# A row of indices placed in PSUM earlier, five banks for the gate's panels, and the level exponentials split over three iterations

## The reference, cut to what matters

```python
def peer_ffn(h, wq, keys, u, v):
    q = (xb @ wq).reshape(PEER_TOKEN_BLOCK, PEER_HEADS, 2, PEER_HALF_DIM)
    s = jnp.einsum('thpd,hpnd->thpn', q, keys)
    s1, i1 = lax.top_k(s[:, :, 0], PEER_TOPK)
    s2, i2 = lax.top_k(s[:, :, 1], PEER_TOPK)
    cand_s = s1[..., :, None] + s2[..., None, :]          # 16 x 16 candidates
    cand_i = i1[..., :, None] * PEER_N_KEYS + i2[..., None, :]
    top_s, pos = lax.top_k(cand_s, PEER_TOPK)
    idx = jnp.take_along_axis(cand_i, pos, axis=-1)
    gate = jax.nn.softmax(top_s, axis=-1)
    act = jax.nn.gelu(jnp.einsum('thkd,td->thk', u[idx], xb))
    return jnp.einsum('thk,thkd->td', gate * act, v[idx])
...
    ffn = peer_ffn(h, peer_wq[i], peer_keys[i], peer_u[i], peer_v[i])
    ple = jax.nn.sigmoid(h @ ple_gate_w[i]) * (p[i] @ ple_w[i])
    h = layer_norm(DEEPNORM_ALPHA * h + ffn + ple, ln2_g[i], ln2_b[i])
```

## Time and profile before

| | us |
|---|---|
| median of 3 runs | 3420.63 (3418.96 to 3421.29) |
| the profiled execution, its own time | 3419.54 |
| its span, first to last instruction | 3417.7 |
| PE busy | 3253.7 |
| DVE busy | 2574.4 |
| ACT busy | 1386.1 |
| POOL busy | 2071.9 |

### The profile page before, as it was taken

The page is one execution under the profiler, slowest core; times in us unless marked ns, Lnnn a source line. Parts: engine busy times, 40 slices in busy tenths (PEclk is TensorE's granted clock), DMA queues, the critical chain, the costliest instruction groups (busy, mean ns, idle before and its releaser), DMA issues. The chain is left out here.

```text
span 3417.7 us, 47046 instructions
## 1 busy us (share of the span) xinstructions
PE 3253.7 (95%) x17370; PEld 2905.1 (85%) x17370; DVE 2574.4 (75%) x4646; ACT 1386.1 (41%) x2698; POOL 2071.9 (61%) x1388
## 2 busy tenths in 40 slices
PE   5999899899999999999989998999999999999996
PEld 4777689899999988888777776899999999888885
DVE  5965359996875588888877733699869666988887
ACT  1235013366666433333212431144666664333332
POOL 5921677666677755555479035766666776555552
PEclk9999899999999999999989998999999999999998
DMA  3310224578899999999723012256888999999994
GB/s 121 94 61 15 95 77 151 195 293 300 296 332 347 350 388 368 363 360 359 254 75 98 32 50 86 75 180 208 295 304 299 344 355 357 384 365 361 361 361 156
DMA packets 312676, 817.12 MB, mean 239 GB/s; under 512 B 22272, under 2 KB 119552, under 8 KB 309120
## 3 DMA queue, kind: packets, MB, share of 16 engines
q1 hardware_dynamic: 112256, 349.02, 29.5%
q0 software_dynamic: 73728, 268.47, 20.2%
q10 hardware_dynamic: 126464, 196.63, 16.5%
HBM read 712.84 MB, written 101.19 MB: 238 GB/s over the span
## 5 line engine op out<-in xcount | busy, mean ns | idle before, releaser
L1239 POOL TENSOR_TENSOR u_lo<-panel,u_hi 128x1024 fp32r<-128x1024 f32 x256 | 629.2, 2459 | 339.8 <-ACT u_hi L1041 335.7
L588 PE MATMUL ps<-hT_hi,u_lo 128*128 128x384 f32 x2048 | 704.6, 344 | 9.1 <-POOL u_lo L1239 9.1
L588 PE MATMUL ps<-hT_lo,u_hi 128*128 128x384 f32 x2048 | 688.1, 336 | 0.0
L588 PE MATMUL ps<-hT_hi,u_hi 128*128 128x384 f32 x2048 | 688.0, 336 | 0.0
L588 PE MATMUL ps<-v_hi,w_lo 128*128 128x512 f32 x1536 | 597.7, 389 | 0.1
L588 PE MATMUL ps<-v_hi,w_hi 128*128 128x512 f32 x1536 | 597.5, 389 | 0.0
L588 PE MATMUL ps<-v_lo,w_hi 128*128 128x512 f32 x1536 | 597.5, 389 | 0.0
L1191 POOL TENSOR_TENSOR ring_hi<-panel,cst 128x512 fp32r<-128x512 f32 x244 | 276.3, 1132 | 441.5 <-PE ps L568 266.0
L1256 POOL TENSOR_TENSOR v_lo<-panel,v_hi 128x1024 fp32r<-128x1024 f32 x128 | 313.4, 2449 | 377.7 <-ACT v_hi L1103 377.6
L1103 ACT CAST v_hi<-panel 128x1024 fp32r<-128x1024 f32 x256 | 269.5, 1053 | 636.3 <-PE ps L588 624.8
L1041 ACT CAST u_hi<-panel 128x1024 fp32r<-128x1024 f32 x256 | 268.2, 1048 | 446.2 <-PE ps L588 441.0
(11 more groups left out here) (260 smaller groups left out, 5733.0 us busy)
## 6 DMA issues: line engine op xcount, KB each, us to landing
panel<-in_u SPq DMA_DIRECT2D x256, 512.0 KB
panel<-in_v SPq DMA_DIRECT2D x256, 512.0 KB
gate_scratch<-arena ACTq DMA_DIRECT2D x24, 2048.0 KB
act_scratch<-arena ACTq DMA_DIRECT2D x124, 384.0 KB
arena<-act_scratch ACTq DMA_DIRECT2D x62, 768.0 KB
arena<-gate_scratch ACTq DMA_DIRECT2D x62, 768.0 KB
panel<-in_w_in SPq DMA_DIRECT2D x28, 1024.0 KB, 5.2
panel<-in_wq SPq DMA_DIRECT2D x16, 1024.0 KB, 5.1
```

The costliest lines, as they stand in the source:

```text
L588: mm = nc.tensor.matmul(o, lhs[a], rhs[b_], start=(start and n == 0), stop=(stop and n == 2))
L1239: pr.mark(nc.gpsimd.tensor_tensor(u_lo[:, j % URING].rearrange("p c n -> p (c n)"), u_tile(j), u_hi[:, j % URING].rearrange("p c n -> p (c ...
```

## The change

Three edits, in both layers.

1. ACT copies `iota` into PSUM bank 3 right after the key scores, ahead of its copy of `x_rows`, and no longer at u tile 6. All four routings compare with `iota_ps`. DVE waits for the copy at the first comparison of each routing.
2. To leave bank 3 alone, the gate's eight outputs go through five banks: 0, 1, 2, 4, 5, 0, 1, 2. The sixth to eighth output wait for the sigmoids of the first to third. The first three u tiles wait for sigmoid 4, 5 and 6 in place of 5, 6 and 7.
3. The seven level exponentials of heads 1 to 3 are seven ACT instructions of 128x512. Levels 1 and 2 stand in the iteration with j % 4 = 1, levels 3, 4, 5 in the next, 6 and 7 in the one after, each right behind `fox_exps(2j)`. DVE signals levels 1 to 4 and 5 to 7 apart, and waits for them apart.

```diff
+SIGMOID_BANKS = (0, 1, 2, 4, 5)
...
+        LOW, HIGH = range(1, 5), range(5, LEVELS)
+        EXP_LEVELS = {1: (1, 2), 2: (3, 4, 5), 3: (6, 7)}
...
-        lev_ready = sig("lev_ready", HH)
-        lev_exp = sig("lev_exp", HH)
+        lev_ready = sig("lev_ready", 2 * HH)
+        lev_exp = sig("lev_exp", 2 * HH)
...
-                def take6(g, release):
+                def take5(g, release):
...
-                    if g >= 6:
-                        pr.need(*freed[g - 6])
+                    if g >= 5:
+                        pr.need(*freed[g - 5])
                     freed.append(release)
-                    return ps[:, g % 6, :]
+                    return ps[:, SIGMOID_BANKS[g % 5], :]
...
                     if j < 3:
-                        pe.wait_ge(gate_sig.sem, layer * gate_sig.per_layer + 5 + j)
+                        pe.wait_ge(gate_sig.sem, layer * gate_sig.per_layer + 4 + j)
...
-                def level_exps(hd):
-
-                    act.wait_ge(lev_ready.sem, layer * lev_ready.per_layer + hd + 1)
-                    for piece in zed_pieces(hd):
-                        last = nc.scalar.activation(piece, piece, ACT.Exp)
-                    pr.mark(last, lev_exp)
-
-                level_exps(0)
+                def level_exps(hd, levels):
+
+                    act.wait_ge(lev_ready.sem, layer * lev_ready.per_layer + 2 * hd + (1 if levels[-1] in LOW else 2))
+                    for lev in levels:
+                        last = nc.scalar.activation(zed(hd, lev), zed(hd, lev), ACT.Exp)
+                        if lev in (LOW[-1], HIGH[-1]):
+                            pr.mark(last, lev_exp)
+
+                act.wait_ge(lev_ready.sem, layer * lev_ready.per_layer + 2)
+                for piece in zed_pieces(0):
+                    last = nc.scalar.activation(piece, piece, ACT.Exp)
+                pr.mark(last, lev_exp, 2)
...
                     if j < NH:
                         fox_exps(2 * j)
+                        if j % NT in EXP_LEVELS and j // NT + 1 < HH:
+                            level_exps(j // NT + 1, EXP_LEVELS[j % NT])
...
-                    if j % NT == 1 and j // NT + 1 < HH:
-                        level_exps(j // NT + 1)
...
                 act.wait_ge(score_sb.sem, layer * score_sb.per_layer + 4 * NT)
+                pr.mark(nc.scalar.copy(iota_ps, iota), iota_ready)
                 pr.mark(nc.scalar.copy(x_rows, h[:, 0, :]), x_ready)
...
-                    pr.mark(nc.scalar.activation(ple_gate[:, i, :], ps[:, g % 6, :], ACT.Sigmoid), gate_sig)
+                    pr.mark(nc.scalar.activation(ple_gate[:, i, :], ps[:, SIGMOID_BANKS[g % 5], :], ACT.Sigmoid), gate_sig)
...
-                    if j == 6:
-                        act.wait_ge(gate_sig.sem, layer * gate_sig.per_layer + 8)
-                        pr.mark(nc.scalar.copy(iota_ps, iota), iota_ready)
...
-                    if levels[-1] == LEVELS - 1:
-                        pr.mark(last, lev_ready)
+                    pr.mark(last, lev_ready)
...
-                    dve.wait_ge(lev_exp.sem, layer * lev_exp.per_layer + hd + 1)
+                    dve.wait_ge(lev_exp.sem, layer * lev_exp.per_layer + 2 * hd + (1 if levels[-1] in LOW else 2))
...
-                        places = iota_ps if i > 1 else iota
+                        if a == 0:
+                            dve.wait_ge(iota_ready.sem, layer * iota_ready.per_layer + 1)
                         step(nc.vector.tensor_tensor(
-                            pick, places[:, 0:CAND].rearrange("p (o c) -> p o c", o=1).to_broadcast([P, TOPK, CAND]),
+                            pick, iota_ps[:, 0:CAND].rearrange("p (o c) -> p o c", o=1).to_broadcast([P, TOPK, CAND]),
...
-                dve.wait_ge(iota_ready.sem, layer * iota_ready.per_layer + 1)
```

More of the change, by code:

```diff
@@ L803, in _ @@
                 freed.clear()
-                def take6(g, release):
+                def take5(g, release):
                     assert g == len(freed), (g, len(freed))
-                    if g >= 6:
-                        pr.need(*freed[g - 6])
+                    if g >= 5:
+                        pr.need(*freed[g - 5])
                     freed.append(release)
-                    return ps[:, g % 6, :]
+                    return ps[:, SIGMOID_BANKS[g % 5], :]
                 pe.wait_ge(score_sb.sem, layer * score_sb.per_layer + 4 * NT)
                 for half in range(2):
-                    project(lambda i: take6(4 * half + i, (gate_sig, 4 * half + i + 1)), True)
+                    project(lambda i: take5(4 * half + i, (gate_sig, 4 * half + i + 1)), True)
                 for j in range(NK):
@@ L1449, in times_keys_queries @@
                         pr.mark(last, z_ready)
-                LOW, HIGH = range(1, 5), range(5, LEVELS)
                 dve.wait_ge(hdec_ready.sem, layer * hdec_ready.per_layer + 1)
```

## The result

The changed kernel takes 3425.77 us (median of 20 runs, 3423.46 to 3432.0) against 3419.68 us (20 runs, 3418.01 to 3421.76): ratio 1.0017, 95% interval 1.0011 to 1.0023. The prediction was 3396. The profiled execution took 3423.66 us, its span is 3421.8.

What follows compares the result with a forecast made beforehand. PE nearly fills the chain; DVE's routing was taken to set PE's two stops per layer. Edit 1's 13.9 us and edit 3's 10.8 gave 24.7 off: 3396, range 3392 to 3400, or 3389 to 3411 with A and B.

Steps and rivals of the forecast that it cites:

- the last one of edit 1: One-hot chunks behind u tile 22: DVE comes some 2.5 us nearer to PE, and nothing is lost.
- the 4.8: Behind the table, both layers: PE's clock stays up after the shorter stop, 2.4 us gained per layer.
- The prediction's own question: Where DVE holds PE: both PE stops, at u tile 17 and behind tile 22, end with an instruction of DVE's routing.
- The mixer: Edit 3, level exponentials: 7.2 us from shorter heads plus 3.6 from the clock, 10.8 in all; bounds 4.8 and 12.
- The table: Routing 1's table, which PE awaits behind tile 22, ready 4.5 us earlier in layer 1, 4.6 in layer 0.
- The sum: Both layers: 13.9 us from edit 1 and 10.8 from edit 3, 24.7 us off.
- Edit 2: Gate outputs through five banks: sigmoids are done in time, so it costs nothing.
- A: Rival: the clock at the table stays half, 19.9 us off, 3400.7; chance 0.2.
- B: Rival: the product takes the whole wait, table only 0.3 us earlier, 3409; chance 0.12.
- C: Rival: the comparison's wait is simply gone, 6.4 us off each routing, 40 us off, 3380; chance 0.05.
- D: Rival: the mixer's level exponentials lie on the path, 8.7 us slower, 3429; chance 0.03.
- the 0.05: Chance left for what the prediction did not see, beside 0.55 for its own forecast.

Runs made afterwards that it cites:

- the later gather: The full change, with POOL gathering a row of u one tile later, so waiting for a dot product one chunk older: 3398.12 us, ratio 0.9932.
- the one whose profiled leads are 4.1 and 4.2 us: The kernel before with two added comparisons on DVE ahead of the first one-hots, 2.0 us per layer: median 3421.46 us, ratio 1.0013.
- the one with 4.1 and 5.0: The kernel before with one added comparison on DVE ahead of the first one-hots, 1.0 us per layer: 3421.21 us, ratio 1.0001.

## Why the prediction was wrong

**The step that failed** is the last one of edit 1: "Behind tile 22 DVE is some 2.5 us nearer to PE. The code lets it make the one-hots two chunks ahead of PE, and I see nothing there to lose; at worst the 4.8 come back." It was 3.3 and 3.5 us nearer, and 28 us were lost. That nothing is lost there holds if every instruction of DVE's keeps its length, for then its work fits PE's pace: with the later gather it takes 95.2 us against 101.0. The prediction does not ask what else waits for DVE there, and puts the loss at nothing without a reason. POOL waits for the dots, and POOL's passes set how long DVE's instructions take. So DVE's lead did not hide DVE's work only; it kept POOL tied to PE. The runs show it from three sides: a delay of 3.1 us in the kernel before sets up the same loss, a gather one tile later removes it in both, and seven of eight products that do not contend remove 9 of its 14 us a layer.

**The prediction's own question was not turned round.** I replayed POOL against DVE, instruction by instruction, in routings 0 and 1, where PE's tiles drive POOL. Routing 2 it does not replay at all, though the earlier trace rows had the product at up to 3.08 us.

**What was right,** against the trace:
- The mixer: 10.8 forecast, 10.9 in the trace (6.2 + 4.7), 12 in the run of edit 3 alone. By layers it is less exact, as I had 5.4 in each. A head takes 24.3 and 24.2 us, 24.3 forecast. PE's stop where the lump was is 0.34 us (1.77 before), and head 0's is 2.1, as forecast.
- The table: 4.5 us (layer 1) and 4.6 (layer 0) forecast, 4.3 and 4.9 measured against the key scores. Routing 0 gives 0.3 us, as forecast: the product takes the wait over. PE's stop at the turn is 1.27 us (1.3), its clock 1.00 behind it; at PE's first one-hots that has given 2.1 and 1.9 us where I had 2.4, after 0.45 of the new wait in each.
- The sum up to the chunks: 24.7 forecast, 23.9 measured. With the gather one tile later, which is another kernel, the whole change gives 3398.12, beside my 3396: the sum was right for all but the chunks.
- Edit 2: no wait of PE's. The first sigmoid is as much earlier as the key scores, 6.2 and 3.6 us; the copy of `x_rows` is 0.2 less early, where I had 0.3.

**The rivals.** None of them was this. A, B and C concern the table; D ended on the right side, at 3429, for a wrong reason: with edit 3 alone the exponentials cost nothing. What happened belongs to the 0.05 that I had left for what I did not see.

## What to carry to other kernels

Before a change brings an engine closer to the one behind it, list every engine that waits for it, not only the one on the path. If one of those also contends with it, its lead is what keeps them apart: here the loss came all at once in a layer, 14.0 us for a lead that is some 3.4 shorter. The remedy is cheap and is not speed: let the follower wait for an older event (here a row place freed a chunk earlier), so that it stays tied to the engine that sets the pace. And where one instruction of a chain stops contending, look at the next one: moving the second operand of the product too gave more (18.9 us) than the edit itself had given by chunk 10 (13.0: 6.7 and 6.3).

## What the runs showed that I had not expected

- One kernel with several times: executions of the one whose profiled leads are 4.1 and 4.2 us took 3420, 3434 or 3446 us. Of the one with 4.1 and 5.0 none of eleven lost anything; with 2.7 and the early gather all did. Where the edge lies is not shown, as the leads of the other executions are not known.
- Small operations pay what is left of a POOL pass as large ones do, up to the whole of it: an addition of 24 elements took 2.41 us in chunk 6, the next of the same size 0.17; the cast of 128x64 took 0.20 us in the kernel before and 1.60 in the changed one; and routing 2's chunks 6, 9 and 18, which hold no 800-element product, are 2.3 to 2.4 us longer than with the later gather.
